# The gate tiles of the first up stage as 512-column products, their halves added by VectorE

## The chip, the cores and the metric

The kernel runs on one core of a Trainium2 chip. The metric is the device time of one execution in microseconds, the median over several runs. Five engines work side by side, each on its own queue in order, and meet at semaphores: TensorE (PE, with its weight loads PEld), VectorE (DVE), ScalarE (ACT), GpSimd (POOL), and SyncE (SP), which issues the loads of the weights.

## The reference

Two blocks of a model over 256 tokens of width 1024, all in fp32. The first is a modulated block: attention with a context, a convolution branch, and a feed-forward part. The second is a macaron block with two SwiGLU feed-forwards and two kinds of attention. What matters here is the feed-forward part of the first:

```
def conv_glu_ffn(h, w_up, dw_w, dw_b, w_down):
    up = h @ w_up                      # 256 x 1024 @ 1024 x 5632
    a, b = jnp.split(up, 2, axis=-1)   # 2816 each
    a = depthwise_conv(a, dw_w, dw_b)  # 3 taps along the tokens
    return (jax.nn.gelu(a, approximate=True) * b) @ w_down
```

The two feed-forwards of the second block compute `(silu(x @ w_gate) * (x @ w_up)) @ w_down` in the same sizes, with no convolution.

## The kernel before, in words

**Split products.** Each fp32 operand of a large product is split in two parts of type fp32r: a high part (a cast) and a low part (operand minus high part). A product is the sum of three: w_hi x_hi, w_hi x_lo, w_lo x_hi. `product` (L628) issues these three. The weights come through a ring of four raw buffers of 1 MB each (`raw`), filled by SP. ScalarE casts a buffer to `whi` (L1280), then VectorE subtracts and writes `wlo` (L1706). `whi` and `wlo` have four slots each. TensorE waits for `lo_done` before it uses a slot, and SP waits for `lo_done` before it fills a raw buffer anew.

**An up stage.** `ffn_up(n)` stands once for each engine, and n is 0, 1, 2 for the three feed-forwards. There are 11 pairs of hidden tiles. A pair is one chunk of gate weights and one chunk of up weights, 256 hidden columns each, so each chunk gives two feature tiles (o = 0, 1) of 128 x 256. The first pair is multiplied whole from the raw buffers (`whole_pair`, L771). The other ten run in a device loop: on PE `chunk(m, q)`, where q = 0 and 2 are gate tiles and q = 1 and 3 are up tiles; on ACT and DVE the loop has `Fori(0, 5)` with two pairs in each turn.

**Two forms of a tile.** An up tile, and in stages 1 and 2 a gate tile too, is made of 512-column products. `xs` holds x's high and low part side by side, so one matmul of `w_hi` against it (L1016) gives w_hi x_hi in columns 0 to 255 and w_hi x_lo in columns 256 to 511 of a bank. Then w_lo x_hi (L1019, 256 columns) is added onto the right half. A tile takes two banks, and somebody has to add the two halves: `add_halves` (L2078), one VectorE reduction from 1024 to 512 columns, which writes to SBUF. In stage 0 the gate tile is made with `product` (L634, L635, L636, 256 columns each) and the three sums land in one place, one bank for both feature tiles.

**What stage 0 does with a gate tile.** ScalarE applies the middle tap and the bias (L1503, two of 256 columns, from the bank to XN). Then it casts the next chunk's weights (`ahead(m, 2 * q)`), waits for VectorE's taps, applies the Gelu (L1509), casts another chunk (`ahead(m, 2 * q + 1)`), waits for h_full and casts the hidden tile (L1517). VectorE adds the two outer taps (L2065, four instructions that read the bank), splits the chunk that ScalarE cast, adds the up tile's halves (L2078, released by PE), multiplies with the Gelu (L2101), splits the second chunk, and writes the low part of the hidden tile (L2072). In stages 1 and 2 there are no taps: VectorE adds the gate tile's halves into FULL and raises `g_sum`, and ScalarE waits for `g_sum` and applies Silu (L1511).

**What sets the order.** Every queue's order is written out by hand. A PE chunk waits for its weights (`lo_done`) and, since each pair uses four banks and there are eight, for `up_sum` of the pair two before. The split that is made in pair p (0 to 9) of the loop is that of the chunks 2p + 4 and 2p + 5 of the stream. For the last two pairs these are the first four chunks of `down0`, the stage behind. `down0` (`token_stage`) multiplies eleven chunks (L631 to L633); ahead of the fifth PE also builds a gate broadcast (L1062) from a diagonal that VectorE writes when its loop is over (L1932).

Of the kernel before, what the change touches and what calls it, by code (L numbers as in the profile page):

```python
# [15 lines left out]
P = 128  # L16
D = 1024
KD = D // P
T = 256
# [10 lines left out]
NPAIR = KF // 2  # L30
# [90 lines left out]
SPLIT, ACC, BANK = {}, {}, []  # L121
# [169 lines left out]
def build(nc, a):  # L291
    ctx = ExitStack()
    with ctx:
# [9 lines left out]
        FULL = sb("FULL", [P, KD, T])  # L303
        xs = sb("x_parts", [P, KD, 2 * T], F32R)
        xhi, xlo = xs[:, :, 0:T], xs[:, :, T:2 * T]
# [53 lines left out]
        acc = ctx.enter_context(nc.psum_tensor("acc", [P, 2 * NR, 512], F32))  # L359
        tp = acc[:, TP:TP + 4, :]  # L360
        s = {n: ctx.enter_context(nc.semaphore(n)) for n in SEMS}
# [15 lines left out]
        def accb(i):  # L377
            return acc[:, BANK[i], :]

        def half(buf, t):  # L380

            flat = buf[:, :, :].rearrange("p a b -> p (a b)")
            return flat[:, t * 512:(t + 1) * 512]
# [9 lines left out]
        for name, j in STREAM:  # L393
            block, _, k = name.partition(".")
# [223 lines left out]
        def _(pe):  # L618
# [9 lines left out]
            def product(out, xh, xl, wh, wl, x_stationary, start, stop):  # L628

                if x_stationary:  # L630
                    pe.matmul(out, xh, wh, start=start, stop=False)  # L631
                    pe.matmul(out, xh, wl, start=False, stop=False)  # L632
                    return pe.matmul(out, xl, wh, start=False, stop=stop)  # L633
                pe.matmul(out, wh, xh, start=start, stop=False)  # L634
                pe.matmul(out, wh, xl, start=False, stop=False)  # L635
                return pe.matmul(out, wl, xh, start=False, stop=stop)  # L636
# [107 lines left out]
            def x_ready(n, b):  # L744
                if n in EDGES:
                    pe.wait_ge(s["bx_lo"], 4 * EDGES[n] + b + 1)
                else:
                    pe.wait_ge(s["xlo"], 4 * ((1, 5).index(n)) + b + 1)
# [243 lines left out]
            def ffn_up(n):  # L992
                si, i = SPLIT[f"up{n}"], ACC[f"up{n}"] + 2

                def chunk(m, q, norm=None):
                    pe.wait_ge(s["lo_done"], si + 4 * m + q + 1)
                    if isinstance(m, int):
                        bank_free(i + q)
                    else:

                        pe.wait_ge(s["up_sum"], (NPAIR - 1) * n + 2 * m + q // 2 - 1)
                    w = [r[(si + q) % NR][:, :].rearrange("p (k n) -> p k n", k=KD) for r in (whi, wlo)]
                    if n == 0 and q % 2 == 0:
                        for o in range(2):
                            for k in range(KD):
                                if norm is not None and o == 0 and k % 2 == 0:
                                    x_ready(norm, k // 2)
                                mm = product(acc[:, BANK[i + q], o * T:(o + 1) * T], xhi[:, k, :], xlo[:, k, :],
                                             w[0][:, k, o * P:(o + 1) * P], w[1][:, k, o * P:(o + 1) * P], False,
                                             k == 0, k == KD - 1)  # L1010
                    else:
                        for k in range(KD):
                            if norm is not None and k % 2 == 0:
                                x_ready(norm, k // 2)
                            for o in range(2):
                                pe.matmul(acc[:, BANK[i + q] + o, :], w[0][:, k, o * P:(o + 1) * P], xs[:, k, :],  # L1016
                                          start=(k == 0), stop=False)
                            for o in range(2):
                                mm = pe.matmul(acc[:, BANK[i + q] + o, T:2 * T], w[1][:, k, o * P:(o + 1) * P],  # L1019
                                               xhi[:, k, :], start=False, stop=(k == KD - 1))  # L1020
                    mm.then_inc(s["acc_ready"], 1)

                whole_pair(f"up{n}", (2, 3, 6)[n])
                for q in range(4):
                    chunk(0, q, (2, 3, 6)[n] if q == 0 else None)
                with pe.Fori(1, 5) as m:
                    for q in range(4):
                        chunk(m, q)
# [243 lines left out]
        def _(act):  # L1272
# [214 lines left out]
            def ffn_up(n):  # L1487
                si, i, c = SPLIT[f"up{n}"], ACC[f"up{n}"], POS[f"up{n}", 0]
                assert n_split[0] == si + 4
                pairs = NPAIR * n  # L1490

                def ahead(m, o):

                    split((si + o) % NR, (c + 2 + o) % NR, 16 * ((c + 2 + o) // NR + 2 + m),
                          ("acc_ready", i + 2 + o + 1 + 4 * m))

                def pair(j, q, first, gate):

                    if n == 0:  # L1500
                        for o in range(2):
                            w = 2 * j + o
                            act.activation(half(XN, q)[:, o * T:(o + 1) * T], gate[:, o * T:(o + 1) * T],  # L1503
                                           ACT.Identity, scale=vt[:, 2, bass.ds(KF + w, 1)],
                                           bias=vt[:, 2, bass.ds(3 * KF + w, 1)]).then_inc(s["cv_act"], 1)
                        if not first:
                            yield
                        act.wait_ge(s["cv_dve"], 4 * j + 4)
                        act.activation(half(XN, 2 + q), half(XN, q), ACT.Gelu_apprx_tanh).then_inc(s["glu_act"], 1)  # L1509
                    else:  # L1510
                        act.activation(half(XN, 2 + q), gate, ACT.Silu).then_inc(s["glu_act"], 1)  # L1511
                        if not first:
                            yield
                    if not first:
                        yield
                    act.wait_ge(s["h_full"], pairs + j + 1)
                    act.copy(hhi[:, bass.ds(2 * j, 2), :],  # L1517
                             half(FULL, q).rearrange("p (o n) -> p o n", o=2)).then_inc(s["h_hi"], 1)

                act.wait_ge(s["acc_ready"], i + 1)  # L1520
                for _ in pair(0, 1, True, accb(i)):
                    pass
                with act.Fori(0, 5) as m:
                    for q in range(2):
                        g = i + 2 + 2 * q
                        if n:
                            act.wait_ge(s["g_sum"], (NPAIR - 1) * (n - 1) + 2 * m + q + 1)
                        else:
                            act.wait_ge(s["acc_ready"], g + 4 * m + 1)
                        for o, _ in enumerate(pair(2 * m + q + 1, q, False, half(FULL, 2 + q) if n else accb(g))):  # L1530
                            ahead(m, 2 * q + o)
                n_split[0] = si + 24

# [148 lines left out]
            for t in range(TT):  # L1682
                for j in (2 * t, 2 * t + 1):
                    i = ACC["gate"] + j
# [8 lines left out]
        def _(dve):  # L1693
# [355 lines left out]
            def ffn_up(n):  # L2049
# [3 lines left out]
                def ahead(m, o):  # L2053
                    split((si + o) % NR, (c + 2 + o) % NR, si + o + 5 + 4 * m)
# [20 lines left out]
                def add_halves(a, m, dst, sem):  # L2075
                    dve.wait_ge(s["acc_ready"], a + 4 * m + 1)
                    parts = acc[:, BANK[a]:BANK[a] + 2, :].rearrange("p o (a n) -> p o n a", a=2)
                    dve.tensor_reduce(dst.rearrange("p (o n) -> p o n", o=2), parts, AX, ALU.add)\  # L2078
                        .then_inc(s[sem], 1)
# [9 lines left out]
                with dve.Fori(0, 5) as m:  # L2089
                    for q in range(2):  # L2090
                        j = 2 * m + q + 1
                        g, u = i + 2 + 2 * q, i + 3 + 2 * q
                        if n:
                            add_halves(g, m, half(FULL, 2 + q), "g_sum")
                        else:
                            taps(j, q, accb(g))
                        ahead(m, 2 * q)
                        add_halves(u, m, half(FULL, q), "up_sum")
                        dve.wait_ge(s["glu_act"], pairs + j + 1)
                        dve.wait_ge(s["up_sum"], (NPAIR - 1) * n + 2 * m + q + 1)  # L2100
                        dve.tensor_tensor(half(FULL, q), half(FULL, q), half(XN, 2 + q), ALU.mult)\  # L2101
                            .then_inc(s["h_full"], 1)
                        ahead(m, 2 * q + 1)
                        low_part(j, q)
# [296 lines left out]
```

## Time and profile before

| | us |
|---|---|
| median of 3 runs (1006.02 to 1006.39) | 1006.28 |
| the profiled execution's own time | 1004.62 |
| its span, first to last instruction | 1002.9 |
| PE busy | 978.2 |
| VectorE busy | 647.3 |
| ScalarE busy | 474.5 |

The profile records one execution. A row of a timeline begins with the start and the length of a group of instructions in us from the span's start. A row of a stretch begins with its bounds and its length, and behind each engine's busy time stands its number of instructions. In a timeline a length is that of one instruction with its latency, so successive instructions overlap a little; distances from start to start tell how fast they follow. The granted clock is a share of full speed (1.00 is 2.4 GHz). The mean granted clock of the whole execution is 0.996.

### The profile page before, as it was taken

How to read it: one execution, taken by the hardware profiler on the slowest of the kernel's cores; microseconds unless marked ns; L12 is line 12 of the kernel's file. 1: busy time of each engine (PE TensorE's matmuls, PEld its weight loads, DVE VectorE, ACT ScalarE, POOL GpSimd, SP SyncE). 2: the span in 40 equal slices, each digit the busy share in tenths (PEclk: the TensorE clock that was granted, in tenths of full speed). 3: DMA queues.
4: the chain of work that ended last, by engine and by line, in shares of the span. 5: the costliest groups of instructions: out<-in, count | busy, mean ns of one | idle time of the engine just before them, and what ended most of it. 6: DMA issues, size and time to landing. Idle time of an engine off the chain costs nothing.

```text
span 1002.9 us, 14911 instructions
## 1 busy us (share of the span) xinstructions
PE 978.2 (98%) x5976; PEld 835.9 (83%) x5976; DVE 647.3 (65%) x840; ACT 474.5 (47%) x624; POOL 49.8 (5%) x89
## 2 busy tenths in 40 slices
PE   5999999999999999999999999999999999999997
PEld 3478877789899999888888888898988988888885
DVE  1278988547669877537677773375355677776354
ACT  3357455574246555334445443158653444444343
POOL 1121100000000000001000000010000100000000
PEclk9999999999999999999999999999999999999999
DMA  9863284764366555550855555255431465555511
GB/s 351 356 252 126 102 319 169 277 248 174 120 229 216 207 196 180 194 184 1 309 203 200 202 208 199 104 202 194 177 111 43 150 248 208 173 208 207 196 56 42
DMA packets 27522, 189.08 MB, mean 189 GB/s; under 512 B 3056, under 2 KB 3312, under 8 KB 5456
## 3 DMA queue, kind: packets, MB, share of 16 engines
q1 hardware_dynamic: 26192, 184.23, 50.1%
q0 software_dynamic: 1136, 4.06, 1.3%
q8 instruction: 37, 0.61, 0.2%
q14 instruction: 13, 0.11, 0.0%
q10 hardware_dynamic: 144, 0.07, 0.0%
HBM read 187.31 MB, written 1.05 MB: 188 GB/s over the span
## 4 chain that ended last, share of the span: by engine, by line
PE 85%; DVE 8%; ACT 2%; DMA 1%; issue 1%; POOL 1%; SPq 0%; DVEq 0%; POOLq 0%; ACTq 0%
PE acc L1016 19%; PE acc L1019 9%; PE acc L631 9%; PE acc L632 9%; PE acc L633 9%; PE acc L634 5%; PE acc L636 5%; PE acc L635 5%; PE acc L771 5%; DVE XN L1901 3%; PE acc L826 3%; DVE wlo L1706 2%; DMA early<-in_early 1%; PE acc L754 1%; PE acc L797 1%
## 5 line engine op out<-in xcount | busy, mean ns | idle before, releaser
L1706 DVE TENSOR_TENSOR wlo<-raw,whi 128x2048 fp32r<-128x2048 f32 x136 | 310.5, 2289 | 152.7 <-ACT whi L1280 152.3
L1280 ACT CAST whi<-raw 128x2048 fp32r<-128x2048 f32 x136 | 256.9, 1906 | 133.0 <-PE acc L633 79.2
L1016 PE MATMUL acc<-x_parts,whi 128*128 128x512 f32 x800 | 251.5, 396 | 0.0
L1019 PEld LDWEIGHTS acc<-x_parts,wlo 128*128 128x128 f32 x800 | 150.3, 188 | 35.5
L1019 PE MATMUL acc<-x_parts,wlo 128*128 128x256 f32 x800 | 157.2, 278 | 0.0
L634 PE MATMUL acc<-x_parts,whi 128*128 128x256 f32 x448 | 128.5, 287 | 1.1 <-DVE FULL L1863 1.1
L636 PE MATMUL acc<-x_parts,wlo 128*128 128x256 f32 x448 | 126.7, 283 | 0.0
L635 PE MATMUL acc<-x_parts,whi 128*128 128x256 f32 x448 | 126.7, 283 | 0.0
L1016 PEld LDWEIGHTS acc<-x_parts,whi 128*128 128x128 f32 x800 | 121.8, 189 | 0.2 <-issue 0.2
L631 PE MATMUL acc<-whi,h_hi 128*128 128x512 f32 x264 | 103.4, 392 | 0.0
L633 PE MATMUL acc<-whi,h_lo 128*128 128x512 f32 x264 | 102.7, 389 | 0.0
L632 PE MATMUL acc<-wlo,h_hi 128*128 128x512 f32 x264 | 102.7, 389 | 0.0
L634 PEld LDWEIGHTS acc<-x_parts,whi 128*128 128x128 f32 x448 | 85.8, 192 | 6.8 <-issue 6.6
L635 PEld LDWEIGHTS acc<-x_parts,whi 128*128 128x128 f32 x448 | 85.9, 192 | 0.3 <-issue 0.2
L636 PEld LDWEIGHTS acc<-x_parts,wlo 128*128 128x128 f32 x448 | 85.8, 192 | 0.0
L2078 DVE TENSOR_REDUCE FULL<-acc 128x512 f32<-128x1024 f32 x50 | 60.9, 1219 | 1.6 <-PE acc L1019 1.6
L631 PE MATMUL acc<-whi,x_parts 128*128 128x512 f32 x144 | 57.3, 398 | 1.6 <-issue 0.8
L771 PE MATMUL acc<-FULL,raw 128*128 128x128 f32 x512 | 58.8, 275 | 0.0
L771 PEld LDWEIGHTS acc<-FULL,raw 128*128 128x128 f32 x512 | 58.1, 192 | 0.5 <-DVE FULL L1764 0.2
L631 PEld LDWEIGHTS acc<-whi,h_hi 128*128 128x128 f32 x264 | 49.6, 188 | 10.4 <-issue 0.2
L633 PEld LDWEIGHTS acc<-whi,h_lo 128*128 128x128 f32 x264 | 49.5, 188 | 10.3
L632 PEld LDWEIGHTS acc<-wlo,h_hi 128*128 128x128 f32 x264 | 49.6, 188 | 10.2 <-issue 0.2
(276 smaller groups left out, 1237.1 us busy)
## 6 DMA issues: line engine op xcount, KB each, us to landing
raw<-in_stream SPq DMA_DIRECT2D x164, 1024.0 KB, 4.9
early<-in_early SPq DMA_DIRECT2D x8, 1024.0 KB, 13.4
X<-in_x SPq DMA_DIRECT2D x2, 512.0 KB, 5.6
G<-in_ctx SPq DMA_DIRECT2D x1, 1024.0 KB, 7.4
bc<-in_g_ffn_post POOLq DMA_DIRECT2D x2, 512.0 KB, 7.0
MX<-in_bias POOLq DMA_DIRECT2D x1, 1024.0 KB, 6.8
out<-X SPq DMA_DIRECT2D x4, 256.0 KB, 2.1
bc<-in_final_g POOLq DMA_DIRECT2D x1, 512.0 KB, 3.7
```

Of the source, the lines that this page charges most:

```text
L631: pe.matmul(out, xh, wh, start=start, stop=False)
L632: pe.matmul(out, xh, wl, start=False, stop=False)
L633: return pe.matmul(out, xl, wh, start=False, stop=stop)
L634: pe.matmul(out, wh, xh, start=start, stop=False)
L635: pe.matmul(out, wh, xl, start=False, stop=False)
L636: return pe.matmul(out, wl, xh, start=False, stop=stop)
L771: mm = pe.matmul(acc[:, BANK[i], o * T + t * P:o * T + (t + 1) * P], w[:, k, o * P:(o + 1) * P], FULL[:, k, t * P:(t + 1) * P], start=(k = ...
L1016: pe.matmul(acc[:, BANK[i + q] + o, :], w[0][:, k, o * P:(o + 1) * P], xs[:, k, :], start=(k == 0), stop=False)
L1019: mm = pe.matmul(acc[:, BANK[i + q] + o, T:2 * T], w[1][:, k, o * P:(o + 1) * P], xhi[:, k, :], start=False, stop=(k == KD - 1))
L1280: act.copy(whi[si_slot][:, :], raw[raw_slot][:, :]).then_inc(s["hi_done"], 1)
L1706: dve.tensor_tensor(wlo[slot][:, :], raw[raw_slot][:, :], whi[slot][:, :], ALU.subtract)\
L2078: dve.tensor_reduce(dst.rearrange("p (o n) -> p o n", o=2), parts, AX, ALU.add)\
```

## The change

Stage 0's gate tiles take the form that all the other tiles of the up stages have: 16 products of 512 columns and 16 of 256, over two banks, for each chunk. VectorE adds the halves into FULL (halves 2 and 3, as in the stages 1 and 2) and raises `g_sum`. ScalarE's affine step in stage 0 waits for `g_sum` in place of PE's `acc_ready`, and it and the taps read FULL in place of the bank. On VectorE the taps move behind the first of the two splits of a pair. The taps of the pair before the loop stay as they are.

```diff
@@ TensorE, chunk(m, q, norm) @@
-                    if n == 0 and q % 2 == 0:
+                    for k in range(KD):
+                        if norm is not None and k % 2 == 0:
+                            x_ready(norm, k // 2)
                         for o in range(2):
-                            for k in range(KD):
-                                if norm is not None and o == 0 and k % 2 == 0:
-                                    x_ready(norm, k // 2)
-                                mm = product(acc[:, BANK[i + q], o * T:(o + 1) * T], xhi[:, k, :], xlo[:, k, :],
-                                             w[0][:, k, o * P:(o + 1) * P], w[1][:, k, o * P:(o + 1) * P], False,
-                                             k == 0, k == KD - 1)
-                    else:
-                        for k in range(KD):
 ...
+                            pe.matmul(acc[:, BANK[i + q] + o, :], w[0][:, k, o * P:(o + 1) * P], xs[:, k, :],
+                                      start=(k == 0), stop=False)
+                        for o in range(2):
+                            mm = pe.matmul(acc[:, BANK[i + q] + o, T:2 * T], w[1][:, k, o * P:(o + 1) * P],
+                                           xhi[:, k, :], start=False, stop=(k == KD - 1))
@@ ScalarE, the loop of ffn_up @@
                     for q in range(2):
-                        g = i + 2 + 2 * q
-                        if n:
-                            act.wait_ge(s["g_sum"], (NPAIR - 1) * (n - 1) + 2 * m + q + 1)
-                        else:
-                            act.wait_ge(s["acc_ready"], g + 4 * m + 1)
-                        for o, _ in enumerate(pair(2 * m + q + 1, q, False, half(FULL, 2 + q) if n else accb(g))):
+                        act.wait_ge(s["g_sum"], (NPAIR - 1) * n + 2 * m + q + 1)
+                        for o, _ in enumerate(pair(2 * m + q + 1, q, False, half(FULL, 2 + q))):
                             ahead(m, 2 * q + o)
@@ VectorE, the loop of ffn_up @@
-                        if n:
-                            add_halves(g, m, half(FULL, 2 + q), "g_sum")
-                        else:
-                            taps(j, q, accb(g))
+                        add_halves(g, m, half(FULL, 2 + q), "g_sum")
                         ahead(m, 2 * q)
+                        if n == 0:
+                            taps(j, q, half(FULL, 2 + q))
                         add_halves(u, m, half(FULL, q), "up_sum")
```

## Rows read from the trace of the kernel before

**Rows 1.** which engines are busy, from the page: busy us (share) x instructions.

```profile
PE 978.2 (98%) x5976; PEld 835.9 (83%) x5976; DVE 647.3 (65%) x840; ACT 474.5 (47%) x624; POOL 49.8 (5%) x89
```

**Rows 2.** stretches: length; PE, PEld, DVE, ACT, POOL busy; granted clock, DMA share, GB/s.

```profile
20.00:25.00 5.00, 5.00 (x20) 2.10 (x13) 0.42 (x1) 0.66 (x2) 0.00 (x0) 0.76 1.01 419
50.00:60.00 10.00, 8.94 (x26) 4.07 (x25) 5.40 (x7) 5.36 (x18) 1.44 (x3) 1.00 0.36 120
339.00:350.50 11.50, 11.50 (x83) 10.79 (x83) 8.85 (x10) 5.99 (x6) 0.00 (x0) 1.00 0.52 182
402.00:602.00 200.00, 199.85 (x1099) 172.18 (x1098) 135.87 (x125) 84.79 (x79) 5.57 (x8) 1.00 0.53 189
```

**Rows 3.** the waits of PE: us in total, times, longest.

```profile
PE acc L631 <- DVE wlo L1706: 0.5, 1, 0.5
```

**Rows 4.** PE's timeline, tiles of up0 and chunks of down0.

```profile
294.68 0.63 PE L1016 MATMUL acc<-x_parts,whi 128*128 128x512 f32 x2
...
300.25 0.28 PE L634 MATMUL acc<-x_parts,whi 128*128 128x256 f32 x1
...
306.01 0.63 PE L1016 MATMUL acc<-x_parts,whi 128*128 128x512 f32 x2
...
402.25 0.40 PE L631 MATMUL acc<-whi,h_hi 128*128 128x512 f32 x1
...
424.04 1.88 PE L1062 MATMUL acc<-FULL,consts 128*128 128x512 f32 x4
```

**Rows 5.** VectorE's timeline in the first up stage.

```profile
302.11 0.69 DVE L2072 TENSOR_TENSOR h_lo<-FULL,h_hi 128x512 fp32r<-128x512 f32 x1 [0.69 <-ACT h_hi L1517]
...
311.17 0.68 DVE L2072 TENSOR_TENSOR h_lo<-FULL,h_hi 128x512 f32 x1
311.77 1.65 DVE L2065 SCALAR_TENSOR_TENSOR XN<-acc,vt,XN 128x255 f32<-128x255 f32 x4
313.33 2.28 DVE L1706 TENSOR_TENSOR wlo<-raw,whi 128x2048 fp32r<-128x2048 f32 x1
315.53 1.22 DVE L2078 TENSOR_REDUCE FULL<-acc 128x512 f32<-128x1024 f32 x1
316.86 0.69 DVE L2101 TENSOR_TENSOR FULL<-FULL,XN 128x512 f32<-128x512 f32 x1
317.46 2.29 DVE L1706 TENSOR_TENSOR wlo<-raw,whi 128x2048 fp32r<-128x2048 f32 x1
...
320.27 1.65 DVE L2065 SCALAR_TENSOR_TENSOR XN<-acc,vt,XN 128x255 f32<-128x255 f32 x4
```

**Rows 6.** ScalarE's timeline in the first up stage.

```profile
309.70 1.02 ACT L1503 ACTIVATE XN<-acc,vt 128x256 f32<-128x256 f32 x2
310.61 1.90 ACT L1280 CAST whi<-raw 128x2048 fp32r<-128x2048 f32 x1
313.45 0.63 ACT L1509 ACTIVATE XN<-XN 128x512 f32<-128x512 f32 x1 [0.94 <-DVE XN L2065]
313.99 1.90 ACT L1280 CAST whi<-raw 128x2048 fp32r<-128x2048 f32 x1
```

**Rows 7.** VectorE's timeline in the second up stage.

```profile
545.74 1.22 DVE L2078 TENSOR_REDUCE FULL<-acc 128x512 f32<-128x1024 f32 x1
549.46 2.29 DVE L1706 TENSOR_TENSOR wlo<-raw,whi 128x2048 fp32r<-128x2048 f32 x1 [2.50 <-ACT whi L1280]
...
556.33 1.22 DVE L2078 TENSOR_REDUCE FULL<-acc 128x512 f32<-128x1024 f32 x1
```

**Rows 8.** ScalarE's timeline in the second up stage.

```profile
546.99 0.63 ACT L1511 ACTIVATE XN<-FULL 128x512 f32<-128x512 f32 x1 [3.22 <-DVE FULL L2078]
547.53 3.70 ACT L1280 CAST whi<-raw 128x2048 fp32r<-128x2048 f32 x2
```

**Rows 9.** taps and convolution taps by line: min/median/max ns, first and last start.

```profile
L2065 DVE SCALAR_TENSOR_TENSOR XN<-acc,vt,XN x44: 471/474/484, 297.0 to 399.4; 128x255 f32<-128x255 f32 x44
...
L1901 DVE SCALAR_TENSOR_TENSOR XN<-conv_x,vt,XN x120: 467/477/482, 79.1 to 178.7; 128x256 f32<-128x256 f32 x120
```

More of the change, by code:

```diff
@@ L1002, in chunk @@
                     w = [r[(si + q) % NR][:, :].rearrange("p (k n) -> p k n", k=KD) for r in (whi, wlo)]
-                    if n == 0 and q % 2 == 0:
+                    for k in range(KD):
+                        if norm is not None and k % 2 == 0:
+                            x_ready(norm, k // 2)
                         for o in range(2):
-                            for k in range(KD):
-                                if norm is not None and o == 0 and k % 2 == 0:
-                                    x_ready(norm, k // 2)
-                                mm = product(acc[:, BANK[i + q], o * T:(o + 1) * T], xhi[:, k, :], xlo[:, k, :],
-                                             w[0][:, k, o * P:(o + 1) * P], w[1][:, k, o * P:(o + 1) * P], False,
-                                             k == 0, k == KD - 1)
-                    else:
-                        for k in range(KD):
[L1013 to L1020, printed above, removed]
+                            pe.matmul(acc[:, BANK[i + q] + o, :], w[0][:, k, o * P:(o + 1) * P], xs[:, k, :],
[3 more added lines that the diff above has]
+                                           xhi[:, k, :], start=False, stop=(k == KD - 1))
                     mm.then_inc(s["acc_ready"], 1)
```

## The prediction, made before the changed kernel was run

> **What bounds the kernel now.** I read the page first: PE is busy for 978.2 us, 98% of the span [rows 1]. Then the busy time by stretches: while the first up stage runs, from 289 to 402 us, PE has no idle time (in the stretch shown, about one pair, 11.50 of 11.50 us, clock 1.00), and VectorE (DVE) is busy 8.85 of 11.50 us [rows 2]. The waits of PE name only 0.5 us lost to VectorE's low parts (L1706) in the whole run [rows 3]. So today the stage costs what its matmuls cost, and everything else in it is hidden. Last I read the timelines of the three engines, since the change puts work on VectorE and ties ScalarE (ACT) to it. I number the ten pairs of the device loop (a gate tile and an up tile each) from 0 to 9, and the tiles that are split for it from 0.
>
> **What TensorE saves.** A gate tile now issues 48 products of 256 columns: from 300.25 to 306.01 it takes 5.76 us. An up tile, with 16 products of 512 columns and 16 of 256, takes 5.57 us (294.68 to 300.25) [rows 4]. After the change every gate tile is an up tile in this respect, so each of ten saves 0.19 us, 1.9 us in all; a pair needs 11.14 us of PE instead of 11.33. The gain is this small because one 512-column product streams as many columns as the two that it replaces. 
>
> **What VectorE gets.** Ten more reductions of 1.22 us (the one it already does for each up tile, `TENSOR_REDUCE`, 315.53) [rows 5]. In busy time this fits: one pair's work repeats every 8.50 us when VectorE waits for nothing (taps at 311.77, next taps at 320.27) [rows 5]; with 1.25 us more it is 9.75, under the 11.14 us of PE. If it were only busy time, the reduction would be hidden.
>
> **Where the wait is added.** It is not only busy time. Today ScalarE's affine step (L1503) waits for TensorE alone. It can be done, with the cast of the next weights behind it, while VectorE still works at the pair before. After the change it waits for g_sum, that is for a reduction which stands in VectorE's queue behind everything of the pair before. Behind the waiting instruction on ScalarE stand: the first cast, the Gelu, the second cast. And VectorE waits in turn for the first cast (its split stands before the taps) and for the second. So the two engines pass one thread of work to and fro, each idle meanwhile. From the start of the reduction, with start-to-start distances:
> - reduction to affine step: 1.25 us (in the second up stage the reduction at 545.74 releases ScalarE at 546.99) [rows 7, 8];
> - two affine steps, to the first cast: 0.91 us (309.70 to 310.61) [rows 6];
> - cast to the split that waits for it: 1.93 us (547.53 to 549.46) [rows 7, 8];
> - split, to what follows: 2.20 us (313.33 to 315.53) [rows 5];
> - four taps and the release of the Gelu: 1.68 us (311.77 to 313.45) [rows 5, 6];
> - Gelu to second cast: 0.54 us (313.45 to 313.99) [rows 6];
> - second cast to second split: 1.93 us as above. Beside it VectorE does the up tile's reduction and the product with the Gelu. From the start of the taps these end at 1.56 + 1.33 + 0.60 = 3.49 us [rows 5], while the split is released at 1.68 + 0.54 + 1.93 = 4.15 us. They are off the path;
> - second split 2.20 us, low part of the hidden tile 0.60 us (311.17 to 311.77) [rows 5]; the next reduction follows.
>
> The sum is 1.25 + 0.91 + 1.93 + 2.20 + 1.68 + 0.54 + 1.93 + 2.20 + 0.60 = 13.24 us for a pair. PE needs 11.14, so the stage is no longer bound by PE, but by this round trip.
> That such round trips are real the second up stage shows. It has the same order without taps, and its period is 1.25 + 0.54 + 1.93 + 2.20 + 1.33 + 0.60 + 2.20 + 0.60 = 10.65 us by the same method; the trace has 10.59 (545.74 to 556.33), with VectorE idle for 2.50 us of each period before the split [rows 7]. There it stays just under PE's 11.14 us and costs nothing. The taps and the longer affine and Gelu steps carry the first stage over that edge.
>
> **What is not in the rows.** The affine step and the taps will read the sums from SBUF (FULL) instead of PSUM. The nearest rows for taps: 0.474 us for 255 columns with one operand in PSUM (L2065), 0.477 us for 256 columns all in SBUF (L1901) [rows 9]. I take no difference, with 0.1 us a pair either way as bounds. For two affine steps from SBUF I take the 0.91 us that they take from PSUM, with -0.1 and +0.2 us as bounds.
> The Trainium skill (VectorE: DVE Perf Modes, The TRN2 errata) gives VectorE 120 fixed cycles with a PSUM source and 58 with SBUF, and ScalarE 172 and 224. By that four taps would be 0.26 us shorter, two affine steps 0.09 us longer, and ten pairs some 1.6 us cheaper. The two tap rows contradict the first half of it; for the second no row stands here.
>
> **Where the end moves.** VectorE comes to the loop at 302.11 + 0.60 = 302.71 us, as now: what stands before is unchanged, and gate tile 0 is ready by 294.7 [rows 4, 5]. Pair p's reduction then starts at 302.71 + 13.24 p. Its first split ends 1.25 + 0.91 + 1.93 + 2.29 = 6.38 us later and releases tile 2p + 4, its second ends 12.73 us later (10.44 + 2.29) and releases tile 2p + 5. Without waits TensorE would start tile 6 at 322.3 and tile 7 at 327.9; the splits release them at 322.3 and 328.7. From there PE waits ahead of each tile, 0.8 and 1.3 us in turn. The stage's last tile (19, pair 7) is released at 408.1 and ends at 413.7, against 402.25 now [rows 4]: 11.5 us. But pairs 8 and 9 split the first four chunks of the down stage, and these come at the same pace. The fourth is released at 302.71 + 9 x 13.24 + 12.73 = 434.6. A chunk there takes 5.45 us ((424.04 - 402.25) / 4), so PE comes to the fifth at 440.05 instead of 424.04 [rows 4]: 16.0 us later. The fifth is not late. ScalarE can cast it as soon as the last hidden tile is cast, and VectorE splits it after the diagonal (about 435.0 + 1.7 + 2.3 = 439.0). From there on the order is the old one.
> Nothing gives this back: from 402 to 602 us PE is busy 199.85 of 200 us [rows 2], so there is no wait that a later start could shorten. The new idle time of PE is 16.0 + 1.9 = 17.9 us. The loads of the weights are released by the splits, move with them, and need no price of their own.
>
> The profiled execution took 1004.62 us around a span of 1002.9, which gives 1020.6. The median of the three runs is 1.66 us above the profiled one, so I predict 1022.3 us, 16.0 us or 1.6% slower. The bounds above make the period 13.0 to 13.6 us, nine periods -2 to +3 us: 1020 to 1025.5 for this case.
>
> **Rivals.**
> - *PE stays the bound* (not slower). If the reduction costs busy time only, VectorE has 9.75 us of work in 11.14, and 1.9 us is saved: 1004.4 us. This decides if the waits on the round trip are under 1.4 us a pair; I work them out as 2.84 us ahead of the first split and 0.66 ahead of the second. For it: the averages, and the same reduction in the second up stage at no price. Against it: the 2.50 us of waiting which that stage shows already, without taps. I give it 8%.
> - *Half of the round trip.* If ScalarE's first cast overlaps with VectorE's work after all (the weights that it casts need only TensorE's release of tile 2p, not the reduction), the period falls by at most 2.84 us, under PE's. With half of it hidden it is 11.8 us, and the end is 9 x 1.4 = 13 us earlier: 1009 us. 6%.
> - *The clock.* PE's new gaps could take its clock from 2.4 to 1.2 GHz. Early in the run, between 20 and 25 us, the granted clock was 0.76; between 50 and 60 us, with PE busy for 8.94 of 10 us, it stayed at 1.00 [rows 2]. The stage would be busy 84%, in gaps of about one microsecond. At half the clock a pair needs some 22.3 us, 9 more than the round trip; for eight pairs 72 us, so 1094. 3%, and less of it more likely than all.
>
> **Numbers.** The round trip has 83%, the rivals 8, 6 and 3. The predicted time is that of the round trip. The range takes in its bounds, some room for handovers that I have not seen together, and a part of the second rival: 1015 to 1027. Two tenths of a per cent, 2.0 us, is what a measurement here can tell. Faster 0.04 and same 0.05 are the first rival (its 1.9 us lies on that edge) with a little of the second; slower has 0.91.
>
> **What would show it.** In the changed kernel's timeline of VectorE the first-stage reductions of gate tiles come 13.2 us apart; the split behind them waits 2.8 us for ScalarE's cast; PE waits for VectorE's low parts ahead of nearly each tile from the seventh on, 17.9 us in all, the first four down chunks included. The tile itself takes 5.57 us. I am wrong if PE has no waits there, if the period is under 12 us, or if the end of the stage moves by 11 us and the down stage adds nothing.

## The result, and the profile after

| | before | changed |
|---|---|---|
| median of 4 runs, us | 1006.15 (1005.92 to 1006.39) | 1026.82 (1025.95 to 1027.9) |
| profiled execution, us | 1004.62 | 1025.95 |
| its span, us | 1002.9 | 1024.2 |

The changed kernel takes 1.0203 times as long, with a 95% interval of 1.019 to 1.0215. That is 20.7 us more, where 16.0 were predicted. The measured time is 4.5 us above the predicted one and 0.2 us below the upper end of the stated range, 1027; two of its four executions lie above that end.

VectorE's timeline of the changed kernel shows one whole pair of the first up stage, from one gate reduction to the next. Its rows answer to [rows 5] and [rows 7]. The line numbers are those of the changed kernel: L2065 is the reduction, L1693 the split, L2052 the taps.

```profile
330.99 1.22 DVE L2065 TENSOR_REDUCE FULL<-acc 128x512 f32<-128x1024 f32 x1
335.37 2.29 DVE L1693 TENSOR_TENSOR wlo<-raw,whi 128x2048 fp32r<-128x2048 f32 x1 [3.16 <-ACT whi L1271]
337.58 1.67 DVE L2052 SCALAR_TENSOR_TENSOR XN<-FULL,vt,XN 128x255 f32<-128x255 f32 x4
339.16 1.22 DVE L2065 TENSOR_REDUCE FULL<-acc 128x512 f32<-128x1024 f32 x1
...
341.74 2.29 DVE L1693 TENSOR_TENSOR wlo<-raw,whi 128x2048 fp32r<-128x2048 f32 x1 [0.56 <-ACT whi L1271]
...
344.55 1.22 DVE L2065 TENSOR_REDUCE FULL<-acc 128x512 f32<-128x1024 f32 x1
```

The period is 344.55 - 330.99 = 13.56 us. In it VectorE stands still twice, for 3.16 and 0.56 us, both times for ScalarE's cast (L1271). ScalarE's timeline of the same pair, where [rows 6] had no wait ahead of the affine step (L1494):

```profile
332.44 1.10 ACT L1494 ACTIVATE XN<-FULL,vt 128x256 f32<-128x256 f32 x2 [3.78 <-DVE FULL L2065]
333.44 1.89 ACT L1271 CAST whi<-raw 128x2048 fp32r<-128x2048 f32 x1
339.28 0.63 ACT L1500 ACTIVATE XN<-XN 128x512 f32<-128x512 f32 x1 [3.94 <-DVE XN L2052]
339.82 1.89 ACT L1271 CAST whi<-raw 128x2048 fp32r<-128x2048 f32 x1
341.61 0.61 ACT L1508 CAST h_hi<-FULL 128x512 f32 x1
```

ScalarE stands still for 3.78 us ahead of the affine step and for 3.94 us ahead of the Gelu. For some 11 of the 13.56 us one of the two engines waits for the other.

TensorE's waits, in total, with the number of times and the longest, are no longer those of [rows 3]:

```profile
PE acc L1007 <- DVE FULL L2065: 11.1, 8, 2.2
...
PE acc L631 <- DVE wlo L1693: 1.0, 2, 0.5
```

And on its timeline the gaps stand ahead of every second tile, the gate tile, with 2.2 and 0.5 us in turn. The second block has the first and the fourth down chunk, and the gate broadcast ahead of the fifth, which in [rows 4] began at 424.04:

```profile
326.97 0.80 PE L1007 MATMUL acc<-x_parts,whi 128*128 128x512 f32 x2 [2.22 <-DVE FULL L2065]
...
340.43 0.74 PE L1007 MATMUL acc<-x_parts,whi 128*128 128x512 f32 x2 [0.52 <-DVE FULL L2065]
...
354.08 0.70 PE L1007 MATMUL acc<-x_parts,whi 128*128 128x512 f32 x2 [2.21 <-DVE FULL L2065]
```

```profile
421.84 0.47 PE L631 MATMUL acc<-whi,h_hi 128*128 128x512 f32 x1 [0.58 <-DVE FULL L2065]
...
438.96 0.50 PE L631 MATMUL acc<-whi,h_hi 128*128 128x512 f32 x1 [0.54 <-DVE wlo L1693]
...
444.54 1.88 PE L1053 MATMUL acc<-FULL,consts 128*128 128x512 f32 x4
```

### The profile page after: what moved, and what is told of

Same layout as the page of the kernel before. It is cut to its first block, busy times and chain, and to the rows that moved or that the text cites. A ratio compares the mean times of both kernels' runs of the same rounds, so it can differ in the third digit from the quotient of the medians.

```text
span 1024.2 us, 14606 instructions
## 1 busy us (share of the span) xinstructions
PE 985.1 (96%) x5816; PEld 832.6 (81%) x5816; DVE 658.2 (64%) x850; ACT 473.2 (46%) x624; POOL 50.2 (5%) x89
## 4 chain that ended last, share of the span: by engine, by line
PE 72%; DVE 12%; ACT 7%; issue 6%; DMA 2%; POOL 1%; DVEq 0%; SPq 0%; ACTq 0%; POOLq 0%
PE acc L1007 15%; PE acc L631 8%; PE acc L632 8%; PE acc L633 8%; PE acc L1010 8%; PE acc L771 5%; ACT whi L1271 4%; PE acc L634 3%; PE acc L636 3%; PE acc L635 3%; DVE XN L1888 3%; PE acc L826 3%; DVE wlo L1693 3%; DMA early<-in_early 2%; DVE XN L2052 1%
## 5 line engine op out<-in xcount | busy, mean ns | idle before, releaser
L1693 DVE TENSOR_TENSOR wlo<-raw,whi 128x2048 fp32r<-128x2048 f32 x136 | 310.3, 2289 | 179.1 <-ACT whi L1271 178.9
L1007 PE MATMUL acc<-x_parts,whi 128*128 128x512 f32 x960 | 307.1, 402 | 11.8 <-DVE FULL L2065 11.1
L1271 ACT CAST whi<-raw 128x2048 fp32r<-128x2048 f32 x136 | 256.5, 1904 | 108.2 <-PE acc L633 69.6
L1010 PEld LDWEIGHTS acc<-x_parts,wlo 128*128 128x128 f32 x960 | 183.4, 191 | 43.7
L1010 PE MATMUL acc<-x_parts,wlo 128*128 128x256 f32 x960 | 191.3, 281 | 0.0
L1007 PEld LDWEIGHTS acc<-x_parts,whi 128*128 128x128 f32 x960 | 148.7, 192 | 13.4 <-issue 9.6
L634 PE MATMUL acc<-x_parts,whi 128*128 128x256 f32 x288 | 83.1, 289 | 1.1 <-DVE FULL L1850 1.1
L636 PE MATMUL acc<-x_parts,wlo 128*128 128x256 f32 x288 | 81.4, 283 | 0.0
L635 PE MATMUL acc<-x_parts,whi 128*128 128x256 f32 x288 | 81.4, 283 | 0.0
L2065 DVE TENSOR_REDUCE FULL<-acc 128x512 f32<-128x1024 f32 x60 | 73.0, 1217 | 0.0
L634 PEld LDWEIGHTS acc<-x_parts,whi 128*128 128x128 f32 x288 | 55.1, 191 | 6.8 <-issue 6.6
L631 PE MATMUL acc<-whi,x_parts 128*128 128x512 f32 x144 | 57.2, 398 | 1.6 <-issue 0.8
L633 PEld LDWEIGHTS acc<-whi,h_lo 128*128 128x128 f32 x264 | 49.6, 188 | 10.4
L633 PE MATMUL acc<-whi,x_parts 128*128 128x512 f32 x144 | 56.1, 390 | 0.0
L632 PE MATMUL acc<-wlo,x_parts 128*128 128x512 f32 x144 | 56.1, 390 | 0.0
```

Of the source, the lines that this page charges most:

```text
L1271: act.copy(whi[si_slot][:, :], raw[raw_slot][:, :]).then_inc(s["hi_done"], 1)
L1693: dve.tensor_tensor(wlo[slot][:, :], raw[raw_slot][:, :], whi[slot][:, :], ALU.subtract)\
```

## The experiments

Each experiment edits the changed kernel unless something else is said. Times are medians. Those of the first four stand beside 1006.46 us for the kernel before, those of the last four beside 1006.44. A ratio is taken to the kernel before, and its interval is the 95% one.

**ScalarE's first cast ahead of the wait.** This takes one of the two casts off the thread and keeps all the work.

```diff
@@ ScalarE, the loop of ffn_up @@
+                        if n == 0:
+                            ahead(m, 2 * q)
                         act.wait_ge(s["g_sum"], (NPAIR - 1) * n + 2 * m + q + 1)
                         for o, _ in enumerate(pair(2 * m + q + 1, q, False, half(FULL, 2 + q))):
-                            ahead(m, 2 * q + o)
+                            if n or o:
+                                ahead(m, 2 * q + o)
```

> The changed kernel, but in the first up stage ScalarE casts the first of the two chunks before it waits for the gate tile's reduction. Round trip (my theory): the cast leaves the path, so does VectorE's wait of 3.16 us ahead of the first split. A pair's period by the measured steps is reduction 1.25, split 2.20, taps and release of the Gelu 1.70, Gelu 0.54, cast 1.93, split 2.20, low part 0.60 = 10.4 us, under TensorE's 11.14. TensorE is the bound again and the 1.9 us of the 512-column products remain: 1004.3 us, 0.2% faster than before. Rival (the price is the banks: TensorE waits for up_sum, as its waits say, and runs at a lower clock after each gap): the up tile's reduction comes 3 us earlier in the pair, but VectorE has as much work; part of the gaps stay, 1010 to 1020 us.

Measured: 1004.64 us, 0.9981 of the kernel before, interval 0.9972 to 0.999. Moving one instruction on one queue gives back all of the loss and leaves the gain. VectorE's timeline of this kernel:

```profile
335.38 1.22 DVE L2068 TENSOR_REDUCE FULL<-acc 128x512 f32<-128x1024 f32 x1
336.51 2.28 DVE L1696 TENSOR_TENSOR wlo<-raw,whi 128x2048 fp32r<-128x2048 f32 x1
338.71 1.66 DVE L2055 SCALAR_TENSOR_TENSOR XN<-FULL,vt,XN 128x255 f32<-128x255 f32 x4
...
342.87 2.29 DVE L1696 TENSOR_TENSOR wlo<-raw,whi 128x2048 fp32r<-128x2048 f32 x1 [0.57 <-ACT whi L1271]
...
345.69 1.22 DVE L2068 TENSOR_REDUCE FULL<-acc 128x512 f32<-128x1024 f32 x1
```

The split follows the reduction without a wait, and the period is 10.31 us (10.4 expected), below TensorE's 11.14. By stretches (length; PE, PEld, DVE, ACT, POOL busy; granted clock, DMA share, GB/s) TensorE has no gap, with VectorE busier than in the changed kernel:

```profile
330.00:390.00 60.00, 60.00 (x346) 52.34 (x345) 55.96 (x57) 35.36 (x36) 0.00 (x0) 1.00 0.57 205
```

**Taps ahead of the first split**, as in the kernel before.

```diff
@@ VectorE, the loop of ffn_up @@
                         add_halves(g, m, half(FULL, 2 + q), "g_sum")
-                        ahead(m, 2 * q)
                         if n == 0:
                             taps(j, q, half(FULL, 2 + q))
+                        ahead(m, 2 * q)
                         add_halves(u, m, half(FULL, q), "up_sum")
```

> The changed kernel, but VectorE's taps stand ahead of the first split again, as in the kernel before. Round trip: VectorE waits about 1.5 us for the affine step instead of 3.16 us for affine step and cast, and the second cast runs beside the first split. Period 2.75 to the taps, 4.41 to the split, 8.54 to the second split, 11.35 us in all: 0.2 us over TensorE's 11.14, with TensorE some microseconds ahead at the start. 1005.2 us, between 1004.3 and 1007. Rival (busy time and banks): the order within VectorE's queue changes nothing in its work, 1020 or more.

Measured: 1006.11 us, ratio 0.9994, interval 0.9984 to 1.0003. The loss is gone here too; the 1.9 us of gain is not resolved. The period in VectorE's timeline is 11.33 us, and the only wait in it is the one for the affine step. That is still above TensorE's 11.14 us, and in the profiled executions about half of the gain is left: from the first gate tile of the loop to the gate broadcast this kernel takes 134.26 us (291.04 to 425.30), the kernel before 135.19, and the one with the cast first 133.33 (290.44 to 423.77).

```profile
327.55 1.22 DVE L2065 TENSOR_REDUCE FULL<-acc 128x512 f32<-128x1024 f32 x1
330.25 1.67 DVE L2052 SCALAR_TENSOR_TENSOR XN<-FULL,vt,XN 128x255 f32<-128x255 f32 x4 [1.48 <-ACT XN L1494]
...
338.88 1.22 DVE L2065 TENSOR_REDUCE FULL<-acc 128x512 f32<-128x1024 f32 x1
```

**The reduction stays, its result unused.** The affine step and the taps read the left halves of the two banks (`left(g)`, in place of FULL), and ScalarE waits for TensorE alone.

```diff
@@ ScalarE and VectorE, n == 0 @@
-                        act.wait_ge(s["g_sum"], (NPAIR - 1) * n + 2 * m + q + 1)
+                            act.wait_ge(s["acc_ready"], g + 4 * m + 1)
 ...
-                        add_halves(g, m, half(FULL, 2 + q), "g_sum")
                         ahead(m, 2 * q)
                         if n == 0:
-                            taps(j, q, half(FULL, 2 + q))
+                            taps(j, q, left(g))
+                            add_halves(g, m, half(FULL, 2 + q), "g_sum")
```

> The changed kernel with every instruction's kind and number kept, but in the first up stage ScalarE's affine step and the taps read the left halves of the gate tile's two banks (the products with x's low part and with the low weights are left out of the gate), ScalarE waits for TensorE alone, and VectorE does the reduction behind the taps, its result unused. Round trip: busy time is the same, the thread is cut, 1004.4 us. Rival (VectorE's 10 x 1.22 us of more work, or its reads of the banks, are the price): 1018 us or more, near the changed kernel.

Measured: 1004.68 us, ratio 0.9976, interval 0.9966 to 0.9986. Ten more reductions on VectorE are free as long as nobody on ScalarE waits for them.

**TensorE's part alone**, put into the kernel before: the matmuls of the change, and `left(g)` in place of `accb(g)` for the affine step and the taps.

> The kernel before with TensorE's part of the change alone: gate tiles of the first up stage as 512-column products over two banks, no reduction; ScalarE's affine step and the taps read the left halves of the banks (the products with x's low part and with the low weights are left out of the gate). It measures the saving by itself. From rows of before 0.19 us for each of ten tiles, 1.9 us: 1004.3 us. By the spacing of N/2.4 + 2.5 ns that the Trainium skill gives (TensorE: Matmul & The Clock Gate, Back-to-back issue gap) it would be 0.4 us: 1005.8 us.

Measured: 1004.29 us, ratio 0.998, interval 0.9971 to 0.9989, that is 2.0 us with an interval of 1.1 to 2.9. It holds the 1.9 us from the rows, and the profiled execution agrees: from the first gate tile to the first down chunk it takes 111.55 us (289.55 to 401.10), the kernel before 113.40 (288.85 to 402.25). By the spacing that the Trainium skill (TensorE: Matmul & The Clock Gate, Back-to-back issue gap) gives for an isolated matmul it would be 0.4, an estimate that lies outside the interval; the section itself says that a stream with weight loads is spaced otherwise.

**The changed kernel again**, for the three that follow.

> The changed kernel once more, beside the three runs of this call: 1026.8 us, so that their differences are taken on one chip.

Measured: 1026.64 us, ratio 1.0202.

**The reduction twice.**

```diff
@@ VectorE, the loop of ffn_up @@
+                        if n == 0:
+                            dve.wait_ge(s["acc_ready"], g + 4 * m + 1)
+                            both = acc[:, BANK[g]:BANK[g] + 2, :].rearrange("p o (a n) -> p o n a", a=2)
+                            dve.tensor_reduce(modrow[:, :].rearrange("p (o n) -> p o n", o=2), both, AX, ALU.add)
                         add_halves(g, m, half(FULL, 2 + q), "g_sum")
```

> The changed kernel, but VectorE does the reduction of each of the ten gate tiles of the first up stage twice, the first time into a spare buffer. Round trip: the reduction stands on the thread, so the period grows from 13.55 by 1.22 to 14.8 us, and nine periods by 11 us: 1037.8 us. Rival (busy time): VectorE would be busy 10.9 us of TensorE's 11.14, the second reduction falls into idle time, 1026.8 us.

Measured: 1038.01 us, ratio 1.0318, interval 1.0301 to 1.0335, 11.4 us above the changed kernel. VectorE's timeline has the same two waits with one more reduction between them:

```profile
333.56 1.22 DVE L2083 TENSOR_REDUCE modrow<-acc 128x512 f32<-128x1024 f32 x1
334.69 1.22 DVE L2065 TENSOR_REDUCE FULL<-acc 128x512 f32<-128x1024 f32 x1
339.06 2.29 DVE L1693 TENSOR_TENSOR wlo<-raw,whi 128x2048 fp32r<-128x2048 f32 x1 [3.15 <-ACT whi L1271]
...
345.42 2.29 DVE L1693 TENSOR_TENSOR wlo<-raw,whi 128x2048 fp32r<-128x2048 f32 x1 [0.56 <-ACT whi L1271]
...
348.23 1.22 DVE L2083 TENSOR_REDUCE modrow<-acc 128x512 f32<-128x1024 f32 x1
```

The period is 14.67 us, 1.11 us more, since two reductions in a row start 1.13 us apart. The path from the loop's first reduction to the last split that matters goes through ten gate reductions, not nine. Ten times 1.11 is 11.1 us.

**Fixed columns in the affine step.** All hidden tiles get the middle tap and bias of the first.

```diff
-                                           ACT.Identity, scale=vt[:, 2, bass.ds(KF + w, 1)],
-                                           bias=vt[:, 2, bass.ds(3 * KF + w, 1)]).then_inc(s["cv_act"], 1)
+                                           ACT.Identity, scale=vt[:, 2, KF:KF + 1],
+                                           bias=vt[:, 2, 3 * KF:3 * KF + 1]).then_inc(s["cv_act"], 1)
```

> The changed kernel, but the affine step takes its scale and bias from fixed columns, not from columns that ScalarE's registers work out for each tile (all hidden tiles get the middle tap and the bias of the first). In the changed kernel the affine step starts 0.26 us after the reduction's end, in the second up stage Silu starts 0.03 us after it. If the register instructions behind the wait are the cause, the period falls by 0.23 us or somewhat more (those between the two affine steps too), nine periods by 2.1 to 3 us: 1024 to 1024.7. If the source in SBUF is the cause, nothing changes: 1026.8.

Measured: 1024.57 us, ratio 1.0177, interval 1.016 to 1.0194, 2.1 us below the changed kernel. The reduction and the affine steps that it releases, from the timelines of VectorE and ScalarE:

```profile
331.18 1.22 DVE L2065 TENSOR_REDUCE FULL<-acc 128x512 f32<-128x1024 f32 x1
335.36 2.29 DVE L1693 TENSOR_TENSOR wlo<-raw,whi 128x2048 fp32r<-128x2048 f32 x1 [2.97 <-ACT whi L1271]
...
344.55 1.22 DVE L2065 TENSOR_REDUCE FULL<-acc 128x512 f32<-128x1024 f32 x1
```

```profile
332.43 1.10 ACT L1494 ACTIVATE XN<-FULL,vt 128x256 f32<-128x256 f32 x2 [3.58 <-DVE FULL L2065]
333.44 1.89 ACT L1271 CAST whi<-raw 128x2048 fp32r<-128x2048 f32 x1
```

The affine step now starts 1.25 us after the reduction's start, against 1.45 in the changed kernel (330.99 to 332.44). The wait ahead of the split is 2.97 instead of 3.16 us, the period 13.37 instead of 13.56. So 0.2 us of each pair are register instructions that ScalarE runs once it has been released: the changed kernel's trace has twenty of them at this line, each about 0.08 us, and the trace of this kernel has none. From the first gate reduction to the last split that matters, ten times 0.19 us is 1.9 us, and the trace has it (132.76 against 130.85 us). But the gate broadcast in the profiled execution comes only 0.9 us earlier, counted from the first gate tile (153.48 against 154.39 us). The first down chunk waits here for the up tile's reduction:

```profile
420.72 0.64 PE L631 MATMUL acc<-whi,h_hi 128*128 128x512 f32 x1 [1.98 <-DVE FULL L2065]
```

Behind this gap the granted clock is 0.83 from 420 to 430 us, and from here to the broadcast at 444.19 TensorE has no more waits: the four chunks take 23.5 us instead of 21.8, and they, not the splits, set the end. The four executions of this kernel lie between 1023.24 and 1025.73 us, and the profiled one is the slowest. So the 0.2 us a pair are shown, and the 2.1 us of the whole run only roughly.

**The up tile's reduction ahead of the taps.**

```diff
@@ VectorE, the loop of ffn_up @@
                         ahead(m, 2 * q)
+                        add_halves(u, m, half(FULL, q), "up_sum")
                         if n == 0:
                             taps(j, q, half(FULL, 2 + q))
-                        add_halves(u, m, half(FULL, q), "up_sum")
```

> The changed kernel, but VectorE adds the up tile's halves ahead of the taps. Then up_sum, for which TensorE's gaps are named, comes 1.6 us earlier within a pair, and the thread through the taps, Gelu and second cast gets 1.25 us longer. Round trip: period 14.8 us, nine periods of +1.25 are 11 us: 1038 us, although TensorE's banks come free earlier. Rival (TensorE is held by the banks): the gap of 2.2 us ahead of each gate tile falls to 0.6, and the clock stays up: 1012 to 1020 us.

Measured: 1037.59 us, ratio 1.0313, interval 1.0296 to 1.033, 11 us above the changed kernel. The period is 347.83 - 333.13 = 14.70 us:

```profile
333.13 1.22 DVE L2065 TENSOR_REDUCE FULL<-acc 128x512 f32<-128x1024 f32 x1
...
339.73 1.22 DVE L2065 TENSOR_REDUCE FULL<-acc 128x512 f32<-128x1024 f32 x1
340.86 1.66 DVE L2052 SCALAR_TENSOR_TENSOR XN<-FULL,vt,XN 128x255 f32<-128x255 f32 x4
...
347.83 1.22 DVE L2065 TENSOR_REDUCE FULL<-acc 128x512 f32<-128x1024 f32 x1
```

TensorE's waits in the changed kernel name the up tile's reduction. Having it earlier in the pair makes the kernel slower, because the taps, and with them the Gelu and the second cast, come later. The waiting engine is not where the time is lost.

## Why the prediction was right, and where it was off

The mechanism was right: the thread, its period, the four down chunks and the order of the waits between VectorE and ScalarE. That the time lies in the stated range owes something to luck. The bounds that the prediction worked out from its terms gave 1020 to 1025.5 us, and 1026.82 lies outside them. The period itself, 13.56 us, is inside its bounds of 13.0 to 13.6. The 4.5 us come from four places, told below: 3.2 us more on the path, 1.3 ahead of the loop, 0.8 behind it, and 0.8 less, since 1.66 us were added from the profiled execution to the median and the changed kernel's two differ by 0.87.

**The saving on TensorE (1.9 us)** was right. TensorE's part alone gave 2.0 us, with 1.85 in its trace.

**Busy time hides the reduction** was right as far as it goes. The kernel with the unused sum has as many reductions and nearly the same busy time on VectorE (657.1 us against 658.2 in the changed kernel), and is faster than before.

**The wait on g_sum makes a round trip longer than TensorE's 11.14 us** was right. The cast moved ahead of the wait, the taps moved ahead of the split, and the reduction taken off the thread each remove the loss. A second reduction, and 1.1 us of other work put into the thread, each lengthen the run by some 11 us. The order of the steps, and VectorE's two waits, are those that the prediction lists. It worked out the waits from distances between starts, as 2.84 and 0.66 us; in the same way the trace has 3.13 and 0.66. The profile's 3.16 and 0.56 count from the end of the instruction ahead, so they are not to be set beside 2.84 and 0.66.

**The terms of the period.** Predicted 13.24 us, measured 13.56, and two terms of the sum carry 0.29 of the 0.32 us. "Reduction to affine step: 1.25 us" measured 1.45. The row it came from was that of Silu, an instruction with no register arithmetic, whereas the affine step's scale and bias columns are worked out by registers behind the wait (shown by the fixed columns, 0.20 us). "Two affine steps, to the first cast: 0.91 us" measured 1.00. They read SBUF instead of PSUM now, and one affine step went from 0.56 to 0.59 us. The kernel with fixed columns still has 1.01 (332.43 to 333.44), so registers are not the reason; the kernel with the unused sum, whose affine steps read PSUM, has 0.91 (334.80 to 335.71), so the source is. The taps kept their length, 1.67 us against 1.65. So of the rule of the Trainium skill (VectorE: DVE Perf Modes, The TRN2 errata) ScalarE's half agrees, by its 52 cycles an estimated 0.04 us for each instruction, and VectorE's half does not.

By source line ScalarE's affine steps of the changed kernel (durations in ns, min/median/max) are:

```profile
L1494 ACTq FUSED_REGOPS  x20: 74/79/84, 305.1 to 427.3; - x20
L1494 ACT ACTIVATE XN<-FULL,vt x20: 584/594/606, 305.3 to 427.8; 128x256 f32<-128x256 f32 x20
...
L1494 ACT ACTIVATE XN<-acc,vt x2: 552/554/555, 297.1 to 297.5; 128x256 f32<-128x256 f32 x2
```

**Where the end moves.** Predicted: from the first gate tile of the loop to the gate broadcast 16.0 us more. Measured: 288.85 to 424.04 before, 290.15 to 444.54 after, 19.2 us more. The prediction's path holds nine periods and the front of the tenth. Each of the nine periods is 0.32 us longer. So is the front: the second split starts 10.75 us after the reduction (330.99 to 341.74) instead of 10.44. Together that is 3.2 us, which is the difference. Four chunks of the down stage are in it, as forecast, and the fourth waits for its split (0.54 us at 438.96, above). The last tile of the up stage alone would not show the loss.

**The rest of the difference.** The two profiled executions differ by 21.3 us. Of it 19.2 are the above. 1.3 us arise ahead of the loop, where both kernels are alike: the first gate tile starts at 290.15 instead of 288.85. A second profiled execution of the changed kernel has 290.73, and the other edits lie between 289.55 and 291.04, so it varies from one execution to the next. The one profiled execution of the kernel before was 1.5 us faster than the median of its four executions, so its 288.85 may be early. The last 0.8 us come after the broadcast. 0.7 of it is one wait of TensorE at the second up stage's entry. All the kernels here whose VectorE does the ten more reductions have it (0.2 to 0.9 us; 0.9 with the first cast ahead), and the two without them, the kernel before and TensorE's part alone, do not. So it comes with the reductions; by which way stays open.

**Which wait TensorE shows** was wrong. "PE waits ahead of each tile, 0.8 and 1.3 us in turn, for the low parts" named the wrong release. The prediction read from the code that a tile waits for up_sum of the pair two before, and then worked out the start from the splits alone. But the up tile's reduction ends 1.45 + 1.00 + 1.93 + 2.21 + 1.58 + 1.22 = 9.4 us into the pair (340.38 in the timeline above), and the first split at 6.7. So every gate tile from the third pair on waits for the reduction, and the up tile behind it finds its weights ready. The first down chunk waits for it too (0.58 us at 421.84). The predicted end did not suffer, since the fourth down chunk waits for its low parts again, as the prediction has it, and the period is set by the thread in either case.

**The clock rival** came true in part, and cost nothing in the changed kernel's profiled execution. The stretches of the changed kernel and of the one with fixed columns (columns as above):

```profile
300.00:440.00 140.00, 127.81 (x663) 108.75 (x661) 100.99 (x106) 62.31 (x64) 0.00 (x0) 0.95 0.44 157
320.00:330.00 10.00, 7.78 (x38) 6.59 (x37) 7.52 (x8) 4.72 (x4) 0.00 (x0) 0.87 0.42 152
330.00:340.00 10.00, 9.91 (x55) 8.46 (x54) 6.84 (x9) 3.62 (x5) 0.00 (x0) 0.96 0.41 134
```

```profile
300.00:440.00 140.00, 123.74 (x667) 105.56 (x666) 102.92 (x113) 63.95 (x65) 0.00 (x0) 0.99 0.45 160
```

In the changed kernel TensorE's granted clock falls to 0.87 in the ten microseconds around a gap of 2.2 us. Single tiles run partly at 1.2 GHz; the tile at 326.97 takes 7.2 us instead of 5.57. TensorE is therefore idle for 12.2 us of the stretch (140 - 127.81) instead of the 17.9 predicted. With fixed columns the gaps are about 2.0 us, the mean clock is 0.99, and TensorE is idle for 16.3 us, yet the period is shorter only by the 0.19 us of the registers. Within the loop a tile at the low clock only fills the gap that would follow it. At its end this need not hold: the low clock behind the wait at 420.72 in the kernel with fixed columns is on the path, and it takes back about 1 of 1.9 us. In the changed kernel the fourth down chunk still waits for its split, so the low clock is off the path. "17.9 us idle" as a sign was therefore off, and the mean clock would have misled.

## What to carry to other kernels

When an instruction is added to a queue that has room, ask first who on another engine waits for it, and what stands behind that waiter. If two in-order queues then release each other several times in each turn of a loop, sum the start-to-start distances along the thread and compare that sum with the bound's period; both engines' busy shares can be low. The cheapest repair is to put ahead of the new wait whatever does not need it: here one line, the cast of the next weights, turns 20.7 us of loss into a gain of 1.8 us (1004.64 against 1006.46 us, ratio 0.9981), the fastest version that computes everything.

The engine that waits longest, and the release its wait names, say where the delay surfaces, not always what to shorten. Having the named reduction earlier cost 11 us here. And a handover must be taken from a row of the same instruction form: here one with register operands starts 0.2 us later after its release.

## What the runs showed of the hardware

- ScalarE's instruction with two columns chosen by registers starts 0.23 us after the end of the reduction that releases it (332.44 against 332.21). With fixed columns it starts 0.03 us after.
- A ScalarE affine step of 256 columns takes 0.594 us from SBUF, and from PSUM 0.554 (two of the same kernel) or 0.562 us (22 of the kernel before). A tap of 255 columns on VectorE takes 0.478 us with both operands in SBUF and 0.474 with one in PSUM.
- In the changed kernel TensorE's gaps are 2.2 and 0.5 us in turn, and the granted clock is 0.95 from 300 to 440 us. With fixed columns they are 1.9 to 2.0 us, one in each 13.4 us, and the granted clock is 0.99 over the same stretch: 1.00 up to 420 us and 0.83 in the ten microseconds behind the last of them.
